# Hybrid decoder layer: every gate ahead of the values, six PSUM banks for the projections, convolution in whole taps with its sums in PSUM

## What is computed

```python
hn = rmsnorm(x, attn_norm_g)
u_a, u_gate, q, k, v, g_out, gk_low = split(hn @ w_in)     # 512, 512, 256, 256, 512, 512, 16
u = u_a * sigmoid(u_gate)
y = causal_depthwise_conv(u, conv_w, width=31) + conv_b    # 512 channels
conv_out = silu(layernorm_over_channels(y) * ln_g + ln_b)
gk = log_sigmoid(gk_low @ gk_w + gk_b) / 16                # forget gates, chunks of 64
gla_out = chunked_gated_linear_attention(q, k, v, gk) -> rmsnorm per head * silu(g_out)
x = x + concat(conv_out, gla_out) @ w_out
x = x + moe(rmsnorm(x))                                    # router, 32 experts, top 2
```

## Times and profile before

| | |
|---|---|
| median of 3 runs | 1180.33 us (1179.59 to 1182.33) |
| profiled execution | 1182.26 us, span 1180.5 us |
| PE busy | 1094.1 us, 93% |
| DVE busy | 987.5 us, 84% |
| ACT busy | 644.0 us, 55% |
| POOL busy | 215.0 us, 18% |
| chain that ended last | PE 78%, DVE 15%, issue 4% |

### The profile page before, as it was taken

The page is one execution under the profiler, slowest core; times in us unless marked ns, Lnnn a source line. Parts: engine busy times, 40 slices in busy tenths (PEclk is TensorE's granted clock), DMA queues, the critical chain, the costliest instruction groups (busy, mean ns, idle before and its releaser), DMA issues.

```text
span 1180.5 us, 14631 instructions
## 1 busy us (share of the span) xinstructions
PE 1094.1 (93%) x5072; PEld 871.4 (74%) x5072; DVE 987.5 (84%) x949; ACT 644.0 (55%) x642; POOL 215.0 (18%) x248
## 2 busy tenths in 40 slices
PE   7999999888989996689999999999999999999954
PEld 5758888666768885568888888888888888888832
DVE  5689799999666666699999999999999999999826
ACT  6433110222652113277777777777777777777612
POOL 0200100121300002312212212222122122222213
PEclk9989999889989998689999999999999999999978
DMA  9420220100222127489999999999999999999646
GB/s 330 110 72 1 72 72 1 36 1 1 86 93 72 55 71 259 166 287 378 360 378 385 377 394 397 387 384 383 369 357 376 379 355 374 368 362 366 243 166 265
DMA packets 68342, 283.00 MB, mean 240 GB/s; under 512 B 11760, under 2 KB 30368, under 8 KB 41424
## 3 DMA queue, kind: packets, MB, share of 16 engines
q1 hardware_dynamic: 54384, 255.95, 58.3%
q0 software_dynamic: 10544, 18.08, 4.3%
q10 hardware_dynamic: 3376, 8.47, 1.8%
HBM read 275.64 MB, written 26.74 MB: 256 GB/s over the span
## 4 chain that ended last, share of the span: by engine, by line
PE 78%; DVE 15%; issue 4%; DMA 1%; ACT 1%; SPq 0%; POOL 0%; POOLq 0%; DVEq 0%; ACTq 0%
PE ps L1780 17%; PE ps L1779 17%; PE ps L1778 16%; DVE acc L1056 7%; PE ps L1773 2%; PE ps L1668 2%; PE ps L1670 2%; PE ps L1669 2%; PE ps L1522 1%; PE ps L1523 1%; PE ps L1524 1%; PE ps L1795 1%; PE ps L1699 1%; PE ps L1579 1%; DVE raw_r L1032 1%
## 5 line engine op out<-in xcount | busy, mean ns | idle before, releaser
L1377 DVE TENSOR_TENSOR w_lo<-raw,w_hi 128x2048 fp32r<-128x2048 f32 x206 | 467.8, 2289 | 52.7 <-ACT w_hi L916 51.0
L916 ACT ACTIVATE w_hi<-raw 128x2048 fp32r<-128x2048 f32 x206 | 392.2, 1919 | 27.9 <-PE ps L1780 27.8
L1778 PE MATMUL ps<-w_hi,xm_hi 128*128 128x512 f32 x560 | 224.6, 401 | 2.6 <-DVE xm_lo L1382 2.5
L1780 PE MATMUL ps<-w_hi,xm_lo 128*128 128x512 f32 x560 | 224.0, 400 | 0.0
L1779 PE MATMUL ps<-w_lo,xm_hi 128*128 128x512 f32 x560 | 223.1, 398 | 0.0
L1056 DVE SCALAR_TENSOR_TENSOR acc<-uT,pcol,acc 128x1024 f32<-128x1024 f32 (+1 forms) x150 | 165.3, 1102 | 4.3
L1778 PEld LDWEIGHTS ps<-w_hi,xm_hi 128*128 128x128 f32 x560 | 106.1, 189 | 27.9 <-DVE xm_lo L1382 3.4
L1779 PEld LDWEIGHTS ps<-w_lo,xm_hi 128*128 128x128 f32 x560 | 106.3, 190 | 25.5
L1780 PEld LDWEIGHTS ps<-w_hi,xm_lo 128*128 128x128 f32 x560 | 106.1, 189 | 23.9
L1778 PE MATMUL ps<-w_hi,hm_hi 128*128 128x512 f32 x280 | 113.0, 404 | 1.8 <-DVE hm_lo L1395 1.5
L1780 PE MATMUL ps<-w_hi,hm_lo 128*128 128x512 f32 x280 | 111.4, 398 | 0.0
(11 more groups left out here) (296 smaller groups left out, 1736.0 us busy)
## 6 DMA issues: line engine op xcount, KB each, us to landing
raw<-in_expert_w_up_dram SPq DMA_DIRECT2D x70, 1024.0 KB, 7.5
raw<-in_expert_w_gate_dram SPq DMA_DIRECT2D x70, 1024.0 KB, 7.2
raw<-in_expert_w_down_dram SPq DMA_DIRECT2D x70, 1024.0 KB, 8.0
raw<-in_w_in_dram SPq DMA_DIRECT2D x8, 1024.0 KB, 7.9
raw<-expert_rows SPq DMA_DIRECT2D x12, 512.0 KB, 8.0
xa<-in_x_dram SPq DMA_DIRECT2D x8, 512.0 KB, 8.7
raw<-in_w_out_dram SPq DMA_DIRECT2D x4, 1024.0 KB, 7.2
xin<-in_x_dram SPq DMA_DIRECT2D x8, 512.0 KB, 3.4
```

Source lines behind the costliest of these rows:

```text
L916: act.activation(w_hi[:, slot, :], raw[:, r, :], ACT.Copy).then_inc(hi_rdy, 1)
L1377: dve.tensor_tensor(w_lo[:, slot, :], raw[:, r, :], w_hi[:, slot, :].bitcast(F32), ALU.subtract)\
L1778: pe.matmul(dst, x_hi, w_hi[:, s, cols], start=first, stop=False)
L1780: return pe.matmul(dst, x_lo, w_hi[:, s, cols], start=False, stop=stop)
```

## The change

Groups 2 and 3 of the gates now stand ahead of the values, so that `N_V` is 22 instead of 14. The channel-wise products from the ninth on, and the values, take turns in banks 0 to 5 (`turn`, `turn_over`, `value_bank`); banks 6 and 7 belong to VectorE, which keeps the running sum of a block there (`wide(6)`) and writes only the last tap of a block to `acc`. All four blocks go in whole taps. The numbers in `conv(...)` are new, and the order of weight pieces, their slots and loads follows the new order. Both halves of the LayerNorm wait for the last tap of all (`conv_done`): means in round 5, variances in round 6, scaling in round 7. `gate_product` has one bank (0) instead of two. The memset of the first state moves from POOL to VectorE, and the copy of `dec` from POOL to ScalarE. Cut to its core:

```diff
         groups = halves("gate", 0) + halves("a", 0) + halves("gate", 1) + halves("a", 1) + halves("low", 0)
         groups += [g for pr in range(PAIRS) for g in halves("gk", pr)]
+        groups += [g for c in (2, 3) for what in ("gate", "a") for g in halves(what, c)]
         N_V = len(groups)
-        groups += [g for c in (2, 3) for what in ("gate", "a") for g in halves(what, c)]
         groups += [g for what in ("q", "k") for c in range(PAIRS) for g in halves(what, c)]
...
+        T_MEAN, T_VAR = 5, 6
...
+        def turn(n):
+
+            return n - 8 if n < N_V else n - 8 + NT
+
         def bank(n):
-
-            return (n if n < N_V else n + NT) % 8
+            return n if n < 8 else turn(n) % 6
+
+        def value_bank(t):
+            return (N_V - 8 + t) % 6
...
+        def turn_over(j):
+
+            j -= 6
+            if j < 0:
+                return tg_dve, j + 7
+            if j < N_V - 8:
+                return tg_dve, j + 9
+            if j < N_V - 8 + NT:
+                return v_rdy, j - (N_V - 8) + 1
+            return tg_dve, j + 9 - NT
...
-        SLOT = {"v0": 2, "v1": 3, "gate2": 0, "a2": 1, "q": 2, "k": 3, "g0": 4, "g1": 5, "o0": 0, "o1": 3, "o2": 4, "o3": 5}
...
+        SLOT = {"v0": 0, "v1": 1, "gate2": 2, "a2": 3, "q": 2, "k": 3, "g0": 4, "g1": 5, "o0": 0, "o1": 3, "o2": 4, "o3": 5}
...
-        CONV = [(c, 0, T) for c in range(CT - 1)] + [(CT - 1, 0, 512), (CT - 1, 512, T)]
-        CONV_0, CONV_1 = CT * TAPS, (CT + 1) * TAPS
+        CONV = [(c, 0, T) for c in range(CT)]
+        N_CONV = CT * TAPS
+
+        def conv_done(eng):
+            eng.wait_ge(conv_step, N_CONV)
...
+            sp.wait_ge(tg_ps, done("a", 1))
             load_piece_in("v0")
             load_piece_in("v1")
-            sp.wait_ge(tg_ps, done("a", 1))
-            load_piece_in("gate2")
-            load_piece_in("a2")
+            sp.wait_ge(tg_ps, done("gate", 3))
+            load_piece_in("q")
+            sp.wait_ge(tg_ps, done("a", 3))
+            load_piece_in("k")
             sp.wait_ge(v_ps, NT)
-            load_piece_in("q")
-            load_piece_in("k")
-            sp.wait_ge(tg_ps, done("gate", 3))
             load_piece_in("g0")
...
-                if t == NT - 3:
+                if t == T_MEAN + 1:
                     centred_squares(0)
-                if t == NT - 2:
+                    centred_squares(1)
+                if t == T_VAR + 1:
                     deviation(0)
+                    deviation(1)
                 if t == NT - 1:
                     conv_out(0)
+                    weights_hi("o0", (n_rdy, HALF))
                     conv_columns(0)
-                    weights_hi("o0", (conv_step, CONV_1))
                     weights_hi("o1")
                 if t + 1 < NT:
                     scaled_keys(t + 1)
                     gate_out(t + 1)
-            centred_squares(1)
...
+                    part = wide(6)[:, lo:hi]
                     for w in range(TAPS):
                         tap = pcol[:, col_w + c * TAPS + w:col_w + c * TAPS + w + 1]
-                        src, dst = uT[:, c, w + lo:w + hi], acc[:, c, lo:hi]
+                        src, dst = uT[:, c, w + lo:w + hi], part if w < TAPS - 1 else acc[:, c, lo:hi]
+                        if n:
+                            dve.wait_ge(conv_step, n)
                         if w == 0:
                             ins = dve.tensor_scalar(dst, src, tap, pcol[:, col_b + c:col_b + c + 1], ALU.mult, ALU.add)
                         else:
-                            dve.wait_ge(conv_step, n)
-                            ins = dve.scalar_tensor_tensor(dst, src, tap, dst, ALU.mult, ALU.add)
+                            if (c, w) == (2, TAPS - 1):
+                                dve.wait_ge(fold_rdy, 2)
+                            ins = dve.scalar_tensor_tensor(dst, src, tap, part, ALU.mult, ALU.add)
...
                 if n == N_V:
-                    weights_lo("gate2")
-                    weights_lo("a2")
-                    conv(52)
+                    conv(4 * 28)
...
-                    conv(12)
+                    conv(4 if h else 12)
...
-                    if c:
-                        conv(4 if c == 1 else 16)
+                    if c == 2:
+                        weights_lo(f"v{h}")
+                    if c > 1:
+                        conv(8)
...
+                    if (c, h) == (1, 1):
+                        conv(12)
+                    elif c > 1:
+                        conv(4)
...
-                    if (c, h) == (0, 1):
+                    if (c, h) == (0, 0):
+                        weights_lo("k")
+                    elif (c, h) == (1, 0):
                         weights_lo("g0")
-                    conv(12)
+                    else:
+                        conv(8)
                 elif what == "k":
                     dve.wait_ge(tg_ps, n + 1)
                     dve.wait_ge(fold_rdy, 2)
                     dve.tensor_tensor(kT[:, c, cols], src, tmp1[:, c, cols], ALU.mult).then_inc(tg_dve, 1)
                     if (c, h) == (0, 0):
                         weights_lo("g1")
-                    conv(14)
+                    else:
+                        conv(8)
...
+                conv_done(dve)
+                dve.tensor_tensor(v, v, ps[:, 6 + h, :].unsqueeze(1).broadcast_to([P, CT, 512]), ALU.subtract)\
...
-                if t == NT - 3:
+                masked(t)
+                if t < T_MEAN:
+                    conv(8)
+                state(t)
+                if t < T_MEAN:
+                    conv(12)
+                else:
+                    conv(4 * N_CONV)
+                if t == T_MEAN:
                     centred(0)
-                masked(t)
-                conv(8)
-                state(t)
-                conv(12)
-                if t == NT - 2:
+                    centred(1)
+                if t == T_VAR + 1:
                     scaled(0)
+                    scaled(1)
                 if t:
                     heads_gated(t - 1)
-                if t == NT - 4:
-                    while sum_conv[0] < CONV_0:
-                        conv(1)
-                elif t == NT - 2:
-                    conv(4 * CONV_1)
-                    dve.wait_ge(conv_step, CONV_1)
-                elif t < NT - 2:
-                    conv(12)
-            centred(1)
+            weights_lo("o0")
             conv_columns_lo(0)
-            weights_lo("o0")
...
-                pe.wait_ge(tg_dve, N_V + t - 7)
+                pe.wait_ge(*turn_over(N_V - 8 + t))
                 tok = slice(t * P, (t + 1) * P)
-                b = (N_V + t) % 8
+                b = value_bank(t)
...
-                if t < 2:
-                    pe.wait_ge(tg_dve, done("q", 0, t))
-                if t >= 2:
-                    pe.wait_ge(g_rdy, t - 1)
+                if t == 0:
+                    pe.wait_ge(tg_dve, groups.index(("q", 1, 0)) + 1)
+                else:
+                    pe.wait_ge(g_rdy, t)
...
-                    last = pe.matmul(rows(6 + t % 2), x_lo_all(k)[:, t, :], w_h, start=False, stop=(k == KC - 1))
+                    pe.matmul(rows(0), xh[:, k, tok], w_h, start=(k == 0), stop=False)
+                    pe.matmul(rows(0), xh[:, k, tok], w_l, start=False, stop=False)
+                    last = pe.matmul(rows(0), x_lo_all(k)[:, t, :], w_h, start=False, stop=(k == KC - 1))
...
-                pe.wait_ge(conv_step, CONV_1 if h else CONV_0)
-                if h:
-                    pe.wait_ge(g_rdy, NT)
+                conv_done(pe)
...
-                if t == NT - 4:
-                    conv_mean(0)
-                if t == NT - 3:
-                    conv_var(0)
-            conv_mean(1)
+                for h in range(HALF):
+                    if t == T_MEAN:
+                        conv_mean(h)
+                    if t == T_VAR:
+                        conv_var(h)
             gla_transposed(0)
             outputs(NT - 1)
             out_projection(0, 0)
-            conv_var(1)
```

More of the change, by code:

```diff
@@ L137, in layer_program @@
         xb_r = at("xb_r", [P, KC - 4, T], F32R, over=o_xb)
-        wv_hi = at("wv_hi", [P, 2, PIECE], F32R, over=o_q)
+        wc_hi = at("wc_hi", [P, 2, PIECE], F32R, over=o_q)
         wq_hi = at("wq_hi", [P, PIECE], F32R, over=o_kT)
@@ L149, in layer_program @@
         lowT = at("lowT", [RANK, T], over=o_kT + 4 * T)
[L150 to L151 removed]
+        sq = [at("sq0", [P, CT, 512], over=o_u), at("sq1", [P, CT, 512], over=o_u + 4 * PIECE)]
+        sdv = [at("sdv0", [P, 512], over=o_u), at("sdv1", [P, 512], over=o_u + 4 * PIECE)]
         wo_hi = at("wo_hi", [P, 2, PIECE], F32R, over=o_u)
@@ L563, in _ @@
                                      pattern=[[1, P]], channel_multiplier=-1))
-            pool.wait_ge(e_rdy, 1)
-            pool.tensor_copy(dec[:], tmp2[:, :, CH - 1:T:CH]).then_inc(dec_rdy, 1)
-            pool.wait_ge(v_ps, NT)
+            pool.wait_ge(tg_ps, done("a", 3))
```

(51 more changed lines are left out.)

61 lines of the change are left out of this document (20 added, 41 removed).

## The result

The changed kernel takes **1219.57 us** (median of 4 runs, 1217.03 to 1223.66) beside 1180.09 us of the kernel before: a ratio of **1.0329**, 95% interval 1.0304 to 1.0353. It is slower by 39.5 us; 40.2 were forecast. Its profiled execution took 1222.04 us, with a span of 1220.3.

The account below looks back on a forecast made before the run. The bound was when `out_projection(0, 0)` starts, set by VectorE's taps: last tap 322 plus tail 50.5 gives 372.5, 43.6 later. Less 3.4 behind it, net 40.2; 1180.33 + 40.2 = 1220.5 us, range 1209 to 1231.

Parts of the forecast that it names:

- The 24 sets of products, banks included, at no cost: TensorE's products ahead of the loop, only reordered, still end at 212 us; 20 us of margin for the banks.
- Loop entry: At the attention loop's start the wait for scaled keys goes, gaining about 4 us; the loop starts at 217.6.
- A tap 1.32 from start to start with its sum in PSUM: VectorE's whole taps cost 1.32 us each, no different with the running sum in PSUM.
- Rivals 1 and 2: First: taps cost more in PSUM, 1224.7 or 1228 us, chance 0.14; second: taps at the opening tap's rate, 1201, chance 0.04.
- 62 x 0.81 beside 31 x 1.32: Last channel block on VectorE: half taps 50 us, whole taps 41, so VectorE is given back 9 us.
- the 0.12 behind the bounds of 1.20 and 1.44: Unexplained excess of a half tap over the 512-column PSUM product, taken as the tap cost's error down and up.
- 59 taps ahead, 25 in the rounds, 40 in one piece: VectorE's queue: 59 taps before `masked(0)`, five in each of rounds 0 to 4, 40 behind `state(5)` taking 52.8 us.
- Idle time of VectorE: Ahead of the loop, about 16 us idle among queries and keys and another 8 before the first query.
- The tail of 50.5 us: From the last tap at 322 to the first output product at 372.5: means, round 6, variances, scaling, output weights.
- Behind it 3.4 us less: After the first output product TensorE no longer has the second half's variance product, 3.4 us less.
- Rival 3: A bank comes late for TensorE's products, costing one set of 5.6 us: 1226 us, chance 0.06.
- Rival 4: Not slower: the 40 taps fit into 12.6 us, 0.31 us a tap, giving 1180 or less, chance 0.02.

Follow-up runs that it names:

- e2_sbuf: The changed kernel with the convolution's running sums in SBUF instead of PSUM banks 6 and 7; 1219.95 us.
- e1_fill: The changed kernel with 18 more taps handed out ahead of the attention loop, where VectorE was idle; 1196.22 us.
- e7_fill_behind: The changed kernel with 18 more taps ahead of the loop, five in each round, the rest and the whole LayerNorm behind the loop; 1185.62 us.
- e5_halves_fill: The changed kernel with block 3 and the LayerNorm in halves and 18 more taps ahead of the loop; 1173.81 us.
- e6_halves_pool: e5_halves_fill with four low-half weight splits on GpSimd and 8 more taps ahead of the loop; 1171.38 us.

## Why the prediction was right

The mechanism and its size were both right; step by step, measured first and forecast in brackets:

- *The 24 sets of products, banks included, at no cost.* Right: TensorE is busy 136.00 of 136 us up to 212 and waits for nothing among the values.
- *Loop entry.* `masked(0)` at 217.77, forecast 218.5. The wait for the scaled keys is gone; the scan-to-loop time fell by 7.7 us.
- *A tap 1.32 from start to start with its sum in PSUM.* Right: 283.09 and 284.42 are successive starts, against 131.09 and 132.41 in the earlier trace rows. Rivals 1 and 2 fall with that, and rival 1 with e2_sbuf as well. The opening tap was not thought of: 1.35 instead of 0.81, one of them among the 40, 0.5 us. The half tap was misread: the 0.81 of the earlier trace rows is a mean with stops beside GpSimd in it, an undisturbed one takes 0.75 (3.09 us for four). So 62 x 0.81 beside 31 x 1.32 compared unlike things, and the 0.12 behind the bounds of 1.20 and 1.44 was too wide. Neither is a term of the sum.
- *59 taps ahead, 25 in the rounds, 40 in one piece.* The rows show the 40; TensorE waited 48.6 us (49 forecast), the last tap ended at 321.5 (322). Round time 9.6 in both.
- *Idle time of VectorE.* 8.3 us ahead of the first query (8), 13.9 among queries and keys (16).
- *The tail of 50.5 us.* 51.0. Two means 9.63 (9.7), round 6 9.6 (9.6), two variances 6.87 (6.9), scores and outputs 3.0 (3.0), head squares, root and the scaling of both halves 14.4 (14.3), the output weights 7.4 (7.0). The low clock had been put into the means alone, from the earlier trace rows, and there it was: the granted clock is 0.56 from 316 to 328 us and 1.00 from 328 to 334, and the means take 9.63 us, the variances 6.87 for as many products.
- *Behind it 3.4 us less.* From the first output product to the end it is 851.6 us before and 847.8 now, 3.8 less.

Rival 3 (a late bank) never showed. Rival 4 asked for 0.31 us a tap, and it was 1.32. That the first output product starts exactly 43.6 us later, as forecast, has some luck in it: counted from the scan it is 44.3, and small errors of both signs (the loop 0.7 early, the opening tap, 0.5 in the tail) cancel.

The right answer had one blind spot: it did not ask what the 40 taps in one piece cost by themselves. Step by step, by the medians, the changed kernel's time falls by 23.4 us when 18 taps move ahead (e1_fill), by another 10.6 when rounds 6 and 7 of TensorE no longer stand behind the last tap (e7_fill_behind), and by 11.8 when block 3 and the LayerNorm go in halves (e5_halves_fill). The front part of the change need not be a loss: with it and 18 more taps ahead, e5_halves_fill beats the kernel before by 8.0 us. Which of the order, the six banks and the sums in PSUM brings how much of that was not taken apart. One part is seen: 60 half taps take VectorE 48.7 us before and 45.3 in e5_halves_fill, where GpSimd stops none of them; how much of that was on the path is not shown.

The forecast weighed a rule of the Trainium skill ("VectorE: DVE Perf Modes", section on the TRN2 errata); as an estimate from its cycle counts, a tap that reads PSUM would take 0.065 us longer. The measurement decides against it here: 1.288 us with the sum in PSUM, 1.300 in SBUF.

## What to carry to other kernels

Moving work of a full engine behind a point where another engine waits was paid 1:1 here, and the idle time it leaves ahead of that point is worth nothing unless filled: count the instructions ahead of and behind the wait on each queue, not their total. Such a wait can cost more than its length: here the products behind it started at the low clock (2.8 us on the two means). Once it is gone, expect the next bound: in e6_halves_pool it took half of the further relief. When a second engine is to work beside the one that updates running sums, look at where the sums lie: in PSUM the taps lost nothing to it here, in SBUF the kernel lost 13.7 to 15.2 us.
